# A hybrid decoder step on one core: the samples' cross attention woven into the prompt's, the first norm and the LRU loop reordered

## The reference

```
h = rmsnorm(x, norm_mix);  u = h @ w_in                    # 10528 columns, split in 11 parts
lru:  xc = conv4(lru_x); r, i = sigmoid(blockdiag(xc)); h = scan(a, u); y = h * gelu(lru_gate)
gla, ssd: two more mixers on other columns of u
x += (g0 * lru @ w_lru_out + g1 * gla @ w_gla_out + g2 * ssd @ w_ssd_out) @ w_mix_out
q = rmsnorm(x, norm_xattn) @ w_xq                          # 4 heads of 256
s = einsum('blhd,bmhd->bhlm', q, k) * 256**-0.5; p = softmax(s); o = einsum('bhlm,bmhd->blhd', p, v)
x += o @ w_xo                                              # k, v: 256 memory tokens
x += (silu(h @ w_ffn_gate) * (h @ w_ffn_up)) @ w_ffn_down;  y = rmsnorm(x, norm_final)
```

## Time and profile before

| | |
|---|---|
| median of three runs | 3195.29 |
| the profiled execution, its span | 3194.77, 3193.0 |
| TensorE busy | 3001.8 (94%) |
| VectorE, ACT, POOL busy | 1186.9 (37%), 719.4 (23%), 824.0 (26%) |
| mean granted TensorE clock | 0.969 |
| DMA | 222.53 MB, 70 GB/s over the span |

### The profile page before, as it was taken

The page is one execution under the profiler, slowest core; times in us unless marked ns, Lnnn a source line. Parts: engine busy times, 40 slices in busy tenths (PEclk is TensorE's granted clock), DMA queues, the critical chain, the costliest instruction groups (busy, mean ns, idle before and its releaser), DMA issues. The chain is left out here.

```text
span 3193.0 us, 41444 instructions
## 1 busy us (share of the span) xinstructions
PE 3001.8 (94%) x17738; PEld 2788.9 (87%) x17738; DVE 1186.9 (37%) x1830; ACT 719.4 (23%) x1302; POOL 824.0 (26%) x493
## 2 busy tenths in 40 slices
PE   5899999999999999989979998988989999999997
PEld 5888999797987999977659987975889999999997
DVE  5777002224233257248732216040152332222224
ACT  3445101123121112235421222142021000000002
POOL 2222222121221233233413225300113233233220
PEclk8999999999999999999989998999999999999998
DMA  3011221212122532222226423104201111111111
GB/s 100 27 36 37 57 75 54 61 47 71 39 71 59 170 104 82 70 80 84 86 68 202 133 71 107 53 7 165 67 27 53 47 40 47 47 40 47 47 40 70
DMA packets 289289, 222.53 MB, mean 70 GB/s; under 512 B 30667, under 2 KB 263180, under 8 KB 289106
## 3 DMA queue, kind: packets, MB, share of 16 engines
q1 hardware_dynamic: 205664, 111.69, 12.6%
q10 hardware_dynamic: 83442, 108.19, 10.3%
HBM read 175.78 MB, written 44.07 MB: 69 GB/s over the span
## 5 line engine op out<-in xcount | busy, mean ns | idle before, releaser
L636 PE MATMUL PS<-Hh,Wh 128*128 128x384 f32 (+1 forms) x2928 | 973.3, 332 | 1.3 <-DVE Hl L2617 1.0
L636 PE MATMUL PS<-Hl,Wh 128*128 128x384 f32 (+1 forms) x2928 | 963.0, 329 | 0.0
L636 PE MATMUL PS<-Hh,Wl 128*128 128x384 f32 (+1 forms) x2928 | 960.1, 328 | 0.0
L576 POOL CAST Wh<-Wr 128x1024 fp32r<-128x1024 f32 x197 | 221.2, 1123 | 2069.8 <-DMA Wr<-in_w_in 858.0
L636 PEld LDWEIGHTS PS<-Hh,Wh 128*128 128x128 f32 x2928 | 552.4, 189 | 3.6 <-DVE Hl L2617 1.1
L578 POOL TENSOR_TENSOR Wl<-Wr,Wh 128x1024 fp32r<-128x1024 f32 x213 | 533.4, 2505 | 81.8 <-ACT Wh L1902 66.0
L636 PEld LDWEIGHTS PS<-Hl,Wh 128*128 128x128 f32 x2928 | 552.4, 189 | 0.6
L636 PEld LDWEIGHTS PS<-Hh,Wl 128*128 128x128 f32 x2928 | 552.0, 189 | 0.0
L2069 DVE SCALAR_TENSOR_TENSOR WK<-WK,PS 128x384 f32<-128x384 f32 (+1 forms) x252 | 133.3, 532 | 882.9 <-PE PS L636 500.5
L2649 DVE TENSOR_TENSOR X<-X,PS 128x384 f32<-128x384 f32 (+1 forms) x288 | 149.6, 531 | 169.9 <-PE PS L1262 90.2
L636 PE MATMUL PS<-Yh,Wh 128*128 128x384 f32 (+1 forms) x576 | 190.9, 331 | 4.8 <-DVE Yl L2342 4.8
(11 more groups left out here) (388 smaller groups left out, 4220.2 us busy)
## 6 DMA issues: line engine op xcount, KB each, us to landing
Wr<-in_w_in SPq DMA_DIRECT2D x82, 512.0 KB, 3.9
merged<-WK ACTq DMA_DIRECT2D x22, 544.0 KB, 3.8
WK<-merged ACTq DMA_DIRECT2D x22, 544.0 KB, 6.2
Wr<-in_w_ffn_gate SPq DMA_DIRECT2D x22, 512.0 KB, 3.8
Wr<-in_w_ffn_up SPq DMA_DIRECT2D x22, 512.0 KB, 3.8
Wr<-in_w_ffn_down SPq DMA_DIRECT2D x22, 512.0 KB, 3.7
WK<-gates ACTq DMA_DIRECT2D x16, 544.0 KB, 5.4
WK<-in_cache_mem_k ACTq DMA_DIRECT2D x8, 1024.0 KB, 4.8
```

The costliest lines, as they stand in the source:

```text
L576: pool.tensor_copy(Wh[:, n % SLOTS], Wr[:, n % SLOTS]).then_inc(w_hi, 1)
L636: mm = pe.matmul(bank(f"{name}:{g}")[:, 0:n], L[:, w % SLOTS, k, :], R[:, k, t0:t0 + n], start=(k == 0 and i == 0), stop=(last and k == DT ...
```

## The change

It has three parts; what is computed stays the same.

1. **First norm.** The x loads are the first DMAs on ACT's queue, with the gain broadcast over 128 partitions (`GAIN`); the vectors, the gate blocks and x from chunk 3 on move to SP's queue behind the first three weight tiles. The gain is multiplied in token-major form, together with the scale, before the turn. ACT and VectorE take the high and low part from PSUM, in halves. The vectors are turned at chunk 2.
2. **LRU loop.** The order on TensorE becomes `lx0`, `lg0`, and then for each t: `lx{t+1}`, `lr{t}`, `li{t}`, `lg{t+1}`. The convolution of t+1 stands on VectorE ahead of the rest of tile t, with two buffers each for its result (`XC`) and for the gate (`GB`).
3. **Cross attention.** The samples go in four pairs. In prompt chunks 0 to 3 the keys of two samples are turned into four ring banks each and copied by ACT and VectorE, half each, into `KTs`. Scores are taken with 32 stationary columns (four samples' tokens, of which 8 are used), head h writing to partitions 32h to 32h+31 of one bank. One pair's softmax is then one 128 x 512 piece of work. In chunks 1 to 4 the pair before is turned, attended in the same way, and turned back. The caches go on SP's queue into six places in `Hh` and `Hl`, which are free from the end of `xq7`. `KTs` and its neighbours lie in the weight slots, so `xo`'s first weights wait for the last pair. `Wh` moves beside `Wr`.

```diff
     for t in range(DT):
-        use([("in", C_LX + t * P)], f"lx{t}")
-        use([("in", C_LG + t * P)], f"lg{t}")
+        if t + 1 < DT:
+            use([("in", C_LX + (t + 1) * P)], f"lx{t + 1}")
         banks(f"lr{t}")
         banks(f"li{t}")
+        if t + 1 < DT:
+            use([("in", C_LG + (t + 1) * P)], f"lg{t + 1}")
...
+        KV_LOADS = [("k", 0, 0, None), ("k", 1, 1, None), ("k", 2, 2, None), ("k", 3, 3, None),
+                    ("v", 0, 4, None), ("v", 1, 5, None),
+                    ("k", 4, 0, "sk0:3"), ("k", 5, 1, "sk1:3"), ("v", 2, 2, "sk2:3"), ("v", 3, 3, "sk3:3"),
+                    ("k", 6, 4, "so0:0"), ("k", 7, 5, "so0:0"), ("v", 4, 2, "so1:0"), ("v", 5, 3, "so1:0"),
+                    ("v", 6, 4, "sk6:3"), ("v", 7, 5, "sk7:3")]
...
+        def KV(i):
+            col = M * (1 + i // 2)
+            return (KVl if i % 2 else KVh)[:, :, col:col + M]
...
+            def load_caches():
+                ready(sp, f"xq{DT - 1}:2")
+                for which, b, i, free in KV_LOADS:
+                    if free:
+                        ready(sp, free)
+                    for m in range(2):
+                        sp.dma_start(KV(i)[:, XH * m:XH * m + XH], I[f"cache_mem_{which}"][0, b, m * P:(m + 1) * P])\
+                            .then_inc(S(f"kv_in{i}"), 16)
             for n, (kind, col, _) in enumerate(WLIST):
+                if n == SLOTS:
+                    first_vectors()
                 if n >= SLOTS:
                     ready(sp, WLIST[n - SLOTS][2])
+                if kind == "xo" and col == 0:
+                    load_caches()
+                    ready(sp, f"sw{PAIRS - 1}:0")
...
+            def sample_scores(b):
+                t0 = first_token(b)
+                if b >= 4 and b % 2 == 0:
+                    pe.wait_ge(S("sp_e"), b // 2 - 1)
+                for h in range(XH):
+                    read(pe, f"sk{b}:{h}")
+                for k in range(2):
+                    for h in range(XH):
+                        mm = pe.matmul(PM[32 * h:32 * h + 32, b // 2 % 2, b % 2 * M:(b % 2 + 1) * M],
+                                       Q[:, 2 * h + k, t0:t0 + 32], KTs[:, b % 2, 2 * h + k, :],
+                                       start=(k == 0), stop=(k == 1))
+                mm.then_inc(S("kb_s"), 1)
...
+            def sample_attend(j):
+                for i in range(2):
+                    for m in range(2):
+                        for h in range(XH):
+                            mm = pe.matmul(bank(name)[32 * h:32 * h + 32, i * XD:(i + 1) * XD],
+                                           PTs[:, 2 * i + m, 32 * h:32 * h + 32], KV(buf)[:, XH * m + h, :],
+                                           start=(m == 0), stop=(m == 1))
...
             for c in range(TT):
                 turn_probs(c)
+                if c < PAIRS:
+                    turn_keys(2 * c)
                 if c + 1 < TT:
                     scores(c + 1)
+                if 1 <= c <= PAIRS:
+                    turn_sample_probs(c - 1)
+                if c < PAIRS:
+                    sample_scores(2 * c)
+                    turn_keys(2 * c + 1)
+                if 1 <= c <= PAIRS:
+                    sample_attend(c - 1)
                 attend(c)
+                if c < PAIRS:
+                    sample_scores(2 * c + 1)
+                if 1 <= c <= PAIRS:
+                    turn_sample_out(c - 1)
...
             for c in range(3):
-                load_x(c)
+                act.dma_start(XS(c), x_rows(c)).then_inc(S(f"x_in{c}"), 16)
+                if c == 0:
+                    act.dma_start(GAIN, I["norm_mix"].broadcast_to([P, D])).then_inc(S("gain_in"), 16)
...
             def scale_x(c):
-                dve.tensor_scalar(wk(5 + c % 2)[0:n, 0:D], XS(c)[0:n], ST[0:n, c:c + 1], None, MUL)\
-                    .then_inc(S("x_scaled"), 1)
+                stt(wk(5 + c % 2)[0:n, 0:D], XS(c)[0:n], ST[0:n, c:c + 1], GAIN[0:n], MUL, MUL).then_inc(S("x_scaled"), 1)
...
             for c in range(TT):
                 turned_probs(c)
+                if c < PAIRS:
+                    copy_keys(2 * c)
                 if c + 1 < TT:
                     probs(c + 1)
+                if 1 <= c <= PAIRS:
+                    turned_sample_probs(c - 1)
+                if c < PAIRS:
+                    copy_keys(2 * c + 1)
                 outputs(c)
+                if c < PAIRS:
+                    sample_probs(c)
+                if 1 <= c <= PAIRS:
+                    sample_outputs(c - 1)
```

More of the change, by code:

```diff
@@ L746, in _ @@
             pe.wait_ge(w_split, 2)
+            pe.wait_ge(masks, NMASK)
             for g in range(len(GROUPS)):
-                pe.wait_ge(S("h_lo"), min(3 * g + 3, TT + 1))
+                for c in range(3 * g, 3 * g + 3):
+                    for i in range(2):
+                        read(pe, f"xt{c}:{i}")
                 for w, name in enumerate(("lx0", "lg0")):
@@ L1176, in _, with turn_sample_out @@
+            def turn_sample_out(j):
+                name = f"sw{j}:0"
+                read(pe, f"so{j}:0")
+                free_bank(pe, name)
+                for i in range(4):
+                    mm = turn(bank(name)[:, i * P:(i + 1) * P], Os[:, i * P:(i + 1) * P], P)
+                done(mm, name)
             scores(0)
@@ L1211, in _ @@
[L1211 to L1223, removed]
-                                       start=(b == 0 and m == 0 and h % 2 == 0), stop=(b == NB - 1 and m == 1),
-                                       skip_group_check=True)
-                    if b == NB - 1 and h % 2:
-                        done(mm, f"{name}:{h // 2}")
-                if b < NB - 1:
-                    mm.then_inc(S("vb"), 1)
@@ L1230, in _ @@
-            for k in range(DT):
-                if k % 4 == 0:
-                    read(pe, f"{name}:{k // 4}")
-                    free_bank(pe, f"xw:{k // 4}")
-                mm = turn(bank(f"xw:{k // 4}")[:, k % 4 * P:k % 4 * P + TS], wk(6)[0:TS, k * P:(k + 1) * P], TS)
-                if k % 4 == 3:
-                    done(mm, f"xw:{k // 4}")
-            read(pe, "xw:0")
-            read(pe, "xw:1")
+                if 1 <= c <= PAIRS:
+                    turn_sample_probs(c - 1)
@@ L1424, in split_x @@
             def split_x(c):
                 n = P if c < TT else TS
-                read(act, f"xt{c}:0")
-                read(act, f"xt{c}:1")
-                act.activation(Hh[:, :, c * P:c * P + n],
-                               wk(7)[:, 0:DT * n].rearrange("p (k t) -> p k t", k=DT), ACT.Copy).then_inc(S("h_hi"), 1)
+                for i in range(2):
+                    ready(act, f"xt{c}:{i}")
+                    act.activation(Hh[:, 4 * i:4 * i + 4, c * P:c * P + n],
+                                   bank(f"xt{c}:{i}").rearrange("p (k t) -> p k t", k=4)[:, :, 0:n], ACT.Copy)\
+                        .then_inc(S("h_hi"), 1)
@@ new lines, in lo_x @@
+            def lo_x(c):
+                n = P if c < TT else TS
+                for i in range(2):
+                    dve.wait_ge(S("h_hi"), 2 * c + i + 1)
+                    ins = dve.tensor_tensor(Hl[:, 4 * i:4 * i + 4, c * P:c * P + n],
+                                            bank(f"xt{c}:{i}").rearrange("p (k t) -> p k t", k=4)[:, :, 0:n],
+                                            Hh[:, 4 * i:4 * i + 4, c * P:c * P + n].bitcast(F32), SUB)
+                    freed(ins, f"xt{c}:{i}")
+                    read(dve, f"xt{c}:{i}")
@@ L2149, in _ @@
-                for i in range(2):
-                    read(dve, f"xt{c}:{i}")
-            lo_x(TT)
+                if c == 2:
+                    ready(dve, "pk0")
+                    freed(dve.tensor_copy(PV[:], bank("pk0")[:, 0:DT * NROW].rearrange("p (k r) -> p k r", k=DT)), "pk0")
+                    ready(dve, "pk1")
+                    freed(dve.tensor_copy(PQ[:], bank("pk1")[:, 0:CT * QROW].rearrange("p (k r) -> p k r", k=CT)), "pk1")
+                if c + 2 <= TT:
+                    scale_x(c + 2)
@@ L2153, in atanh_of @@
+                lo_x(c)
+            read(dve, "pk0")
+            read(dve, "pk1")
             def atanh_of(e, s, s2, p):
```

393 lines of the change are left out of this document (227 added, 166 removed).

## The result

| | median us | runs | lowest to highest |
|---|---|---|---|
| before, same chip | 3196.87 | 4 | 3190.13 to 3200.14 |
| changed | 3083.1 | 4 | 3081.79 to 3086.08 |

The ratio is 0.9648 (95% interval 0.963 to 0.9666). The forecast was 3103 in a range of 3084 to 3138. In a second set the changed kernel took 3081.4 against 3195.25.

A forecast was written before the change was run, and what follows sets the result against it. The prediction took TensorE, busy 94% of the span, to bound the kernel. Its terms gave 3194.8 - 13 - 22 - 58 = 3101.8 us, stated as 3103 for a little clock given back, range 3084 to 3138.

The forecast's parts named there:

- first norm: Stage before the first projection: earlier x loads and a shorter pace per chunk gain 13 us.
- LRU: LRU loop and its end: the new order removes TensorE's waits, a net gain of 22 us.
- attention: Cross attention: samples interleaved with prompt chunks, scores in overlapping column quarters, cut 185.9 to 127.1 us, a gain of 58.
- chunk 0 of the attention: First prompt chunk of cross attention: 15.1 us plus 3 for the half clock at its start, given as 18.5.
- the landing of x3: First norm: x3, loaded after the vectors on SP, lands about 17 us and holds chunk 3's scale until about 19.5.
- 28.7: LRU loop: us lost to TensorE's waits (23.0) and the slow clock behind them, all taken as gained.
- LRU's end: After the LRU loop: a new wait of 5 us before `lt`, and 1 more for the banks of `low`.
- Rival A: Cross attention: column quarters don't overlap, or only in pairs; 3138 us if serial, about 3120 in pairs; chance 0.17.
- B: LRU loop: bound by VectorE and ACT handing over, period 30 us instead of 27.9, 3119 in all; chance 0.10.
- C: Caches or x arrive late: TensorE waits in chunks 2 and 3, 5 us per late pair, about 3115; chance 0.11.
- The rule weighed there: Cross attention scores: weight loads overlap products only in different row groups, so column quarters run serially, 3.5 us a sample.
- Rival D: Cross attention: TensorE's clock stays at 1.2 GHz through the whole interleaved stage, making the kernel slower, 3238 us; chance 0.04.

The follow-up runs named there:

- x-on-ACT run: The changed kernel with the loads of x tiles 3 and later issued by ACT instead of SP; 3082.26 us.
- in the last: Changed kernel plus reordered end of the LRU, x loads on ACT, vectors turned at tile 5, sample 0's keys turned before the first prompt probabilities; 3074.11 us.
- the quarters' probe: The changed kernel with eight extra products before each sample's scores, on one, two or four column quarters or two halves; 3095.14 us in one run.

## Why the prediction was right, and where it was not

By the stretches the terms came out at 8.7 for 13 (first norm), 23.7 for 22 (LRU), 65.6 for 58 (attention) and 14.5 for nothing (the stretches between and behind them). So in the three edited stages the mechanisms were right; two sizes were off, and by chance the norm's shortfall hid part of the attention's excess; and one term was missing. The missing one, `Wh`'s offset, is worth 9.7 by the medians; without it the time would have been about 3093, within the range. With it the time fell just below a lower end that had added up the best case of every part. One sum in the working is off: chunk 0 of the attention, 15.1 plus 3, is 18.1 and not 18.5, which changes nothing.

**First norm: the landing of x3 was mis-sized, and so was what it holds up.** The step said that x3 lands about 17 and the first projection starts at 36; they came at 21.4 and 40.66. Timeline of the changed kernel:

```profile
4.19 4.42 SPq L574 DMA_DIRECT2D WK<-in_lru_conv_w  x1
...
10.09 1.94 PE L796 MATMUL PS<-ident,WK 128*128 128x128 f32 x8 [10.09 <-DVE WK L2189]
...
16.77 11.78 SPq L594 DMA_DIRECT2D WK<-in_x_prompt  x5
18.53 4.18 PE L796 MATMUL PS<-ident,WK 47*128 47x47 f32 x26 [3.45 <-DMA WK<-in_ssd_conv_b]
21.47 1.06 ACT L1529 ACTIVATE YA<-WK 128x1024 f32<-128x1024 f32 x1 [7.81 <-DMA WK<-in_x_prompt]
...
33.95 1.97 PE L796 MATMUL PS<-ident,WK 128*128 128x128 f32 x8 [0.88 <-DVE WK L2189]
36.79 1.97 PE L796 MATMUL PS<-ident,WK 128*128 128x128 f32 x8 [0.87 <-DVE WK L2189]
```

The first turn (10.09; forecast 10) and the pace (2.85 from 33.95 to 36.79; forecast 3.0) were right. Missed: SP's first small DMA alone occupies its queue from 4.19 for 4.42 us, so the issues end at 16.75 and x3 is issued only then. But the x-on-ACT run shows that the late issue was not the only cause: issued 5.7 us sooner, x3 lands only 1.9 sooner, and most of that is lost to POOL. VectorE sets this stage: scale, low part and reciprocal make the 2.85 a tile.
The Trainium skill, "SBUF — State Buffer", section "Who interferes with whom", says that a VectorE instruction with two SBUF inputs contends with a GpSimd instruction that reads SBUF, and that the loser blocks. The trace agrees: the scale has two such inputs, x and the gain, and takes 2.93 to 3.18 us beside POOL's subtractions and 1.28 after them. In three kernels it ends 1.08 us behind the subtraction (24.27 after 23.19 with x on ACT, 16.34 after 15.26 in the changed kernel, 24.16 after 23.08 in the last).

**LRU loop: right.** 32.5 gained for 28.7, its period 27.35 for "near 28", no waits in it. The 28.7 had counted only what was lost. Most of the rest is the faster projection: 220.95 less eight pairs of small products at 3.82 and 1.8 for the slow start leaves 11.78 each for sixteen, against 11.97, 3.0 us. The offset explains 0.11 of the 0.19 each, 1.8 us (xq2 to xq7 take 71.17 instead of 71.81 with `Wh` moved alone, 71.71 when it is moved 32 bytes further); what the other 1.2 comes from no run shows. One period of the loop, from `lr2` to `lr3` (27.35):

```profile
132.89 3.82 PE L811 MATMUL PS<-WK,YA 128*128 128x384 f32 x12
160.24 3.82 PE L811 MATMUL PS<-YA 128*128 128x384 f32 x12
```

**LRU's end: the size right (8.8 for 6), the place wrong.** The wait stands before `low` and not before `lt`:

```profile
263.45 1.11 ACT L1588 ACTIVATE Yh<-WK 128x1088 fp32r<-128x1088 f32 x1 [5.03 <-DVE WK L2189]
264.47 1.09 ACT L1567 ACTIVATE WK<-WK 128x1088 f32<-128x1088 f32 x1
265.58 1.28 ACT L1421 ACT_TABLE_LOAD   x1
266.88 1.47 ACT L1421 ACTIVATE WK<-PS,SC 128x384 f32<-128x384 f32 x3
267.60 0.66 PE L734 MATMUL PS<-Hh,Wh 128*128 128x384 f32 x1 [5.99 <-ACT WK L1421]
```

`lr7` and `li7` fill all six banks, and ACT frees the first only at 266.88 plus a third of 1.47, behind tile 6's Yh copy, tile 7's square and a table load. The prediction gave these banks 1 us. Behind the wait of 5.99 the clock is low (0.83 over the stretch), and the same work takes 14.63 where it took 11.81: 2.8 more. With both, `low` ends so late that nothing is left to wait for before `lt`.

**Attention: right in mechanism, too careful in size (65.6 for 58).**

```profile
2049.34 1.07 PE L1304 MATMUL PM<-KTs,Q 128*32 128x256 f32 x16
...
2073.98 1.04 PE L796 MATMUL PS<-ident,WK 128*128 128x128 f32 x8
...
2091.76 1.04 PE L796 MATMUL PS<-ident,WK 128*128 128x128 f32 x8
...
2094.80 0.66 PE L796 MATMUL PS<-ident,KVh 128*128 128x128 f32 x4 [0.69 <-DVE Hl L2778]
```

Scores of a sample 1.0 (forecast 1.3; see the earlier trace rows, from which it was taken), a chunk of 17.8 (2073.98 to 2091.76) for 19.7, the bank wait 0.69, chunk 4's wait on the turned probabilities 3.07 for 3.2, no wait on a cache load, 120.4 in all for 127.1. Rival A is dead by the quarters' probe, B by the period of 27.35, C by the absence of cache waits; the part of C that spoke of x came true in small, in the norm's late x3.
The rule weighed there, that weight loads overlap only for different row groups (the Trainium skill, "TensorE: Matmul & The Clock Gate", Part 3), would have given 3.5 a sample by the prediction's working; 1.0 here, and 0.9 for four quarters against 3.3 for a single one in the probe, decide against it for columns. The Trainium skill's "TensorEngine Tiling (Array Packing)" states that different tiles of the array load and multiply in parallel, and with that the trace agrees.

**Rival D: wrong in price, alive in small.** The clock did not stay low through the stage: it was 0.94 over all, and 1.00 from 2046.7 to 2106.7, where most of the turns of keys stand. But see the last section.

**What had no step at all** was the move of `Wh`: 9.7 us by the medians, a tenth of the forecast gain. This is the term that failed by being absent: the diff showed it, I had read it as bookkeeping, and the prediction says that everything outside the three stages keeps its time.

## What to carry to other kernels

When a diff moves a buffer, work out its byte offset before and after: here 32 bytes past a multiple of 64 made TensorE's weight products of 384 columns 1% longer, 9.7 us in all, and no row of the trace before points at it. After a change, subtract the stretches whose code is untouched first; what they gain or lose is what no theory of the edited stages can explain. And before a transfer is made earlier, ask which neighbour its first use will then run beside: of about two us of earlier landing most was lost to POOL, twice.

## What the runs showed of the hardware

**A wait of 3 us sometimes costs the clock, sometimes not.** Two executions of the changed kernel, chunk 4's wait of 3.07 and the stretches behind it (columns as above; the clock is the third figure from the end). The first:

```profile
2117.54 1.93 PE L1326 MATMUL PS<-KVh,PTs 128*32 128x256 f32 x16 [3.07 <-ACT PTs L2101]
...
2117.60:2118.60 1.00, 1.00 (x12) 0.53 (x16) 0.94 (x1) 0.00 (x0) 0.00 (x0) 0.50 0.00 0
2120.00:2122.00 2.00, 2.00 (x16) 1.08 (x9) 0.69 (x1) 0.00 (x0) 0.00 (x0) 0.50 0.00 0
```

The repeat:

```profile
2120.00 1.07 PE L1326 MATMUL PS<-KVh,PTs 128*32 128x256 f32 x16 [3.07 <-ACT PTs L2101]
...
2120.00:2121.00 1.00, 1.00 (x20) 0.66 (x24) 1.00 (x1) 0.00 (x0) 0.00 (x0) 1.00 0.00 0
2122.50:2124.50 2.00, 2.00 (x20) 2.00 (x19) 0.20 (x1) 0.55 (x1) 0.00 (x0) 1.00 0.00 0
```

Same program, same wait; half clock (1.2 GHz) in one, full (2.4) in the other, and the stage takes 120.4 or 117.3 us. In the run with the old norm it took 125.0. Executions of the changed kernel lie 4 to 6 us apart, and 3 us in one stage can hide gains of that size. How much of the scatter comes from here no run parts: the repeat, 3.1 us faster in this stage, was 3.1 slower between the LRU and the attention.

**The clock's row can be wrong at the start.** The first stretch says 1.00, yet eight turns take 1.94 there against 1.04 in the attention. In the kernel before they take 1.97 at 40.87, in the stretch whose clock is 0.50. So the engine ran at half speed; read the durations beside the row.

What the offset does inside TensorE, and why chunk 4's wait tips the clock only at times, stays open.
